# Strip matmuls of a decoder step that read and write their columns in backward order

## The reference

```python
h = rmsnorm(x, norm1_g)
z = h @ w_in                       # 2048 -> 18448 columns
u, cg, bg, q, k, v, o, gif, g_a, g_b = split(z)
a_out = bg * causal_dwconv(cg * u, state, w_shortconv)
hb = mlstm(q, k * DK ** -0.5, v, gates(gif), state)       # 8 heads
mix = sigmoid(g_a) * a_out + sigmoid(g_b) * sigmoid(o) * hb
x = x + mix @ w_out                # 2048 -> 2048
up = causal_dwconv(rmsnorm(x, norm2_g) @ w_up, state, w_ffconv)   # 2048 -> 11264
x = x + (silu(up[..., D_FF:]) * up[..., :D_FF]) @ w_down          # 5632 -> 2048
y = rmsnorm(x, norm_f_g)
```

## Time and profile before

| | before |
|---|---|
| runs | 1708.65 us median of 3 (1707.38 to 1709.73) |
| profiled execution, span | 1706.3 us |
| TensorE (PE) busy | 1695.1 us, 99% |
| VectorE (DVE) busy | 1200.1 us, 70% |
| ScalarE (ACT) busy | 766.5 us, 45% |
| GpSimd (POOL) busy | 479.6 us, 28% |
| read from and written to HBM | 305.09 MB and 12.78 MB |

### The profile page before, as it was taken

The page is one execution under the profiler, slowest core; times in us unless marked ns, Lnnn a source line. Parts: engine busy times, 40 slices in busy tenths (PEclk is TensorE's granted clock), DMA queues, the critical chain, the costliest instruction groups (busy, mean ns, idle before and its releaser), DMA issues.

```text
span 1706.3 us, 37177 instructions
## 1 busy us (share of the span) xinstructions
PE 1695.1 (99%) x13726; PEld 1688.7 (99%) x13726; DVE 1200.1 (70%) x1901; ACT 766.5 (45%) x916; POOL 479.6 (28%) x501
## 2 busy tenths in 40 slices
PE   9999999999999999999999999999999999999997
PEld 8999999999999999999999999999999999999997
DVE  5875957667595766759688877777555777777554
ACT  6545435354443535444444554544333334334443
POOL 4422414242141424215343222222000222222220
PEclk9999999999999999999999999999999999999999
DMA  8787786868778586877866666656666666666663
GB/s 204 183 230 197 201 212 155 225 162 231 188 198 212 156 226 163 230 189 199 196 178 182 185 175 175 180 173 173 183 181 181 181 178 179 176 180 177 183 176 119
DMA packets 591165, 318.80 MB, mean 187 GB/s; under 512 B 17684, under 2 KB 585988, under 8 KB 588988
## 3 DMA queue, kind: packets, MB, share of 16 engines
q1 hardware_dynamic: 578564, 292.99, 63.2%
q10 hardware_dynamic: 10448, 21.57, 4.7%
q0 software_dynamic: 2064, 2.92, 0.8%
HBM read 305.09 MB, written 12.78 MB: 186 GB/s over the span
## 4 chain that ended last, share of the span: by engine, by line
PE 99%; ACT 0%; POOL 0%; DVE 0%; issue 0%; ACTq 0%; POOLq 0%; DVEq 0%
PE strip L1528 32%; PE strip L1520 32%; PE strip L1524 32%; PE aux L1399 1%; PE aux L1407 1%; PE strip L1451 0%; PE aux L1581 0%; PE aux L1471 0%; PE strip L1464 0%; PE aux L1611 0%; PE aux L1610 0%; PE aux L1624 0%; PE strip L1399 0%; PE aux L1615 0%; PE aux L1608 0%; PE aux L1616 0%
## 5 line engine op out<-in xcount | busy, mean ns | idle before, releaser
L978 DVE TENSOR_TENSOR w_lo<-w_raw,w_hi 128x1024 fp32r<-128x1024 f32 x556 | 723.1, 1303 | 315.3 <-ACT w_hi L709 314.8
L709 ACT ACTIVATE w_hi<-w_raw 128x1024 fp32r<-128x1024 f32 x557 | 586.1, 1059 | 756.7 <-PE strip L1528 724.7
L1520 PE MATMUL strip<-xh,w_hi 128*128 128x268 f32 (+1 forms) x3424 | 493.1, 286 | 0.0
L1528 PE MATMUL strip<-xh,w_lo 128*128 128x268 f32 (+1 forms) x3424 | 492.4, 286 | 0.0
L1524 PE MATMUL strip<-xl,w_hi 128*128 128x268 f32 (+1 forms) x3424 | 492.0, 286 | 0.0
L1528 PEld LDWEIGHTS strip<-xh,w_lo 128*128 128x128 f32 x3424 | 449.4, 188 | 0.3
L1520 PEld LDWEIGHTS strip<-xh,w_hi 128*128 128x128 f32 x3424 | 449.4, 188 | 0.2
L1524 PEld LDWEIGHTS strip<-xl,w_hi 128*128 128x128 f32 x3424 | 449.4, 188 | 0.0
L680 POOL TENSOR_TENSOR gg<-sg,cz 128x264 f32<-128x264 f32 x44 | 57.1, 1297 | 415.8 <-ACT sg L923 415.8
L1520 PE MATMUL strip<-hh,w_hi 128*128 128x264 f32 x704 | 102.2, 286 | 0.0
L683 POOL TENSOR_TENSOR hid<-gg,cz 128x264 f32<-128x264 f32 x44 | 73.5, 1670 | 102.2 <-DVE cz L1327 102.2
(11 more groups left out here) (324 smaller groups left out, 1285.3 us busy)
## 6 DMA issues: line engine op xcount, KB each, us to landing
w_raw<-in_w_in SPq DMA_DIRECT2D x256, 512.0 KB, 4.4
w_raw<-in_w_up SPq DMA_DIRECT2D x176, 512.0 KB, 3.9
w_raw<-in_w_down SPq DMA_DIRECT2D x64, 512.0 KB, 3.9
w_raw<-in_w_out SPq DMA_DIRECT2D x32, 512.0 KB, 4.4
w_raw<-in_w_down SPq DMA_DIRECT2D x32, 384.0 KB, 3.3
out<-c_st ACTq DMA_DIRECT2D x8, 1024.0 KB, 7.2
c_st<-in_state_mlstm_C ACTq DMA_DIRECT2D x7, 1024.0 KB, 10.5
rb<-scratch_rows ACTq DMA_DIRECT2D x8, 270.0 KB, 5.0
```

Source lines behind the costliest of these rows:

```text
L709: act.activation(w_hi[:, slot, :], w_raw[:, slot, :], ACT.Copy).then_inc(hi_done, 1)
L978: v.tensor_tensor(w_lo[:, slot, :], w_raw[:, slot, :], w_hi[:, slot, :].bitcast(f32), ALU.subtract).then_inc(lo_done, 1)
L1520: pe.matmul(bank[b][:, 0:c1 - c0], w_hi[:, slot, w], rh[:, k0 + k, c0:c1], start=(first and k == 0), stop=False)
L1528: mm = pe.matmul(bank[b][:, 0:c1 - c0], w_lo[:, slot, w], rh[:, k0 + k, c0:c1], start=False, stop=(last and k == kk - 1))
```

## The change

In all matmuls of the strips, the moving operand and the output are given with a step of minus one: the instruction reads the last column of its moving rows first, and writes the last column of its output first. Each output column gets the same products as before. The stationary operand, the order of the instructions, waits and transfers are not changed, nor are the matmuls into auxiliary banks.

```diff
--- before.py
+++ after.py
@@ -1448,7 +1448,7 @@
                     pe.wait_ge(xl_done, k + 1)
                     w = slice(k % KU * P, (k % KU + 1) * P)
                     for t, xt in enumerate((xh, xl)):
-                        mm = pe.matmul(bank[s][:, 0:NT - c0], w_hi[:, 2 * s + k // KU, w], xt[:, k, c0:NT],
+                        mm = pe.matmul(bank[s][:, 0:NT - c0][:, ::-1], w_hi[:, 2 * s + k // KU, w], xt[:, k, c0:NT][:, ::-1],
                                        start=(k == 0 and t == 0), stop=False)
                 return mm
 
@@ -1461,8 +1461,8 @@
                     pe.wait_ge(lo_done, RING + 2 * (s + 1))
                 for k in range(lo, hi):
                     pe.wait_ge(xh_done, k + 1)
-                    mm = pe.matmul(bank[s][:, 0:NT - c0], w_lo[:, 2 * s + h, (k - h * KU) * P:(k - h * KU + 1) * P],
-                                   xh[:, k, c0:NT], start=False, stop=(last and k == KT - 1))
+                    mm = pe.matmul(bank[s][:, 0:NT - c0][:, ::-1], w_lo[:, 2 * s + h, (k - h * KU) * P:(k - h * KU + 1) * P],
+                                   xh[:, k, c0:NT][:, ::-1], start=False, stop=(last and k == KT - 1))
                 return mm
 
             def gates(lo, hi):
@@ -1517,15 +1517,15 @@
                         if at_k == k:
                             pe.wait_ge(sm, value)
                     w = slice(k * P, (k + 1) * P)
-                    pe.matmul(bank[b][:, 0:c1 - c0], w_hi[:, slot, w], rh[:, k0 + k, c0:c1],
+                    pe.matmul(bank[b][:, 0:c1 - c0][:, ::-1], w_hi[:, slot, w], rh[:, k0 + k, c0:c1][:, ::-1],
                               start=(first and k == 0), stop=False)
                 for k in range(kk):
                     w = slice(k * P, (k + 1) * P)
-                    pe.matmul(bank[b][:, 0:c1 - c0], w_hi[:, slot, w], rl[:, k0 + k, c0:c1], start=False, stop=False)
+                    pe.matmul(bank[b][:, 0:c1 - c0][:, ::-1], w_hi[:, slot, w], rl[:, k0 + k, c0:c1][:, ::-1], start=False, stop=False)
                 pe.wait_ge(lo_done, u + 1 + RING)
                 for k in range(kk):
                     w = slice(k * P, (k + 1) * P)
-                    mm = pe.matmul(bank[b][:, 0:c1 - c0], w_lo[:, slot, w], rh[:, k0 + k, c0:c1],
+                    mm = pe.matmul(bank[b][:, 0:c1 - c0][:, ::-1], w_lo[:, slot, w], rh[:, k0 + k, c0:c1][:, ::-1],
                                    start=False, stop=(last and k == kk - 1))
                 if frees:
                     mm.then_inc(unit_used, frees)
```

## The result

The changed kernel takes 1712.05 us, median of 14 runs (1711.08 to 1712.91); the kernel before took 1708.83 us beside it (14 runs, 1707.38 to 1710.89). The ratio is 1.0017, with a 95% interval of 1.001 to 1.0024: 3.2 us more. That is inside the 0.2% named as "no change", but close to its edge: the interval does not contain 1, and its upper end lies beyond the 0.2%.

The account below looks back on a forecast made before the run. The prediction took TensorE's pace from one strip matmul to the next as the bound; terms 0 + 0 + 0 left the span at 1706.3 us, so it forecast 1708.7 us for the runs, range 1,696 to 1,730 us.

Parts of the forecast that it names:

- no change: Whole kernel: time stays within 0.2%, 3.4 us, of the kernel before; chance 0.54.
- half rate: Rival, all strip matmuls: falling order handles one word at a time, in full 3,286 us; chance 0.20.
- upper bound of 119 ns a matmul: Strip matmuls: most a backward stream could add, falling to the rate of unrounded operands; 1,577 us over 13,248 matmuls.
- 8-byte rule: PSUM writes: lines hold 8 bytes and any access pattern that is not contiguous slows matmuls significantly.
- second reading: PSUM writes: every two consecutive elements should be contiguous; turned pairs stay in one line, so the sum would be 0.
- 0 + 0 + 0: Whole kernel: order between matmuls, edges and backward stream each cost 0, so the span stays at 1706.3 us.
- the turned stream itself: Strip matmuls' backward read and write: taken as 0, between a gain of at most 13 us and a 1,577 us cost.
- cover that I named: Strips of 264 to 268 columns: a cycle or two at a row's start may hide; at 280 it would show.
- small cost: Rival, 9,600 strip matmuls at 122 ns: each pays 2.1 ns, 20.2 us more, 1,729 us; chance 0.14.
- quick pace throughout: Rival: first up pass leaves 124 ns for 122, 5.2 us less, 1,703 us; with wide strips 1,696; chance 0.12.
- main step: Forecast of no change: strip starts 122 or 124 ns apart at 268 columns, 128.75 at 280, same 13,726 instructions.
- Edges: Strips' moving rows and banks: widths and starts are even, so backward reads cover the same word pairs; cost 0.

Follow-up runs that it names:

- output_only: Kernel before with only the strips' output columns written backwards, moving rows read forwards: 1708.71 us against 1708.68, ratio 1.0002 (0.9993 to 1.0011).

## Why the prediction was right, point by point

**The bound.** TensorE's row set the time before and after: it is busy for 99% of the span in both, and its list of waits is the same.

**No half rate.** The upper bound of 119 ns a matmul was not approached; the largest change of any stage is about 2 ns. The 8-byte rule that I weighed is thus settled for this case in the second reading: by the runs a backward write costs nothing, 1.0002 (0.9993 to 1.0011). The Trainium skill, page "Advanced Engine Details and Errata", section "PSUM Cachelines", asks that every two consecutive elements be contiguous, and the output_only trace agrees that a step of minus one meets that, with 121.7 ns in the output strips as before.

The 241 ns behind that upper bound was misread: it is the length of a piece of the chain divided by 12, and not a distance between starts. The twelve f32 matmuls and the first strip matmul behind them start here:

```profile
9.80 2.96 PE L1407 MATMUL aux<-acc,ones 128*128 128x266 f32 x12
...
12.40 0.48 PE L1451 MATMUL strip<-xh,w_hi 128*128 128x268 f32 x1
```

That is 2.60 / 12 = 217 ns, so the bound was about 95 ns a matmul, some 1,260 us in all. The rival stays as far off as it was.

**The sum 0 + 0 + 0.** It came out at 3.2 us, 0.24 ns a matmul, a hair under the 0.26 that I had set as its border. The term "the turned stream itself" was mis-sized as one number: it is +0.5 ns in the heads' strips behind the score matmuls, +0.35 in the wide strips, +2 in the output strips, -0.9 in the first up pass, +1.2 in the second, and +0.2 and 0 in the two passes of down strips. That the total is near zero is partly a cancelling of stages, and so far it was luck: without the 1.7 us that the first up pass gave back, the change would have cost 4.9 us, 0.29%. The cover that I named (cycles hidden at 264 to 268 columns) held only for 264, nearly. The row it was read from does not show a cover either: the transposes at 110 ns work on f32 operands, and if 266 such columns take 217 ns, 128 come to 104 ns (an estimate), so their columns may explain most of it. And the column per cycle was read from the slower of the two paces at 268 columns; from 122.1 ns the step to 280 columns is 0.55 ns a column.

**The two small rivals.** I gave them as cases that exclude each other, a small cost (0.14) and the quick pace throughout (0.12). Each happened in part, in different stages: the second up pass and the output strips became slower; the first up pass became quicker, though at 123.3 ns and not at 122. So did the strips ahead of the score matmuls, 0.99 us for 8 before; in the changed kernel's chain they read:

```profile
152.82 0.98 PE strip L1528 x8
```

Nor did the sign come that I had named for the main step, starts of 268 columns 122 or 124 ns apart: the turned strips have paces of their own, 122.5 and 123.3. The sentence on which the second rival was turned down, that the pace changes where the instruction mix changes and the turn leaves that alone, failed: the same mix leads turned strips into other paces, and in the second head before the pace changes where the mix does not.

**Edges.** "Reading the same pairs of words" was not enough for a forward read: two words' shift alone moved it by 0.8 ns. But it is not what the backward read pays for: turned, the same shift left 124.0 ns.

**What is shown and what is open.** Shown: the read alone makes the difference; each shape and direction has a few paces (268 columns: 122.0 and 124.2 forward, 122.5 and 123.3 turned); a stage keeps its pace for hundreds of matmuls; one wide f32r matmul can change it, and so can a stop of about 0.1 us, behind which two executions of one program differ. Not shown: what in TensorE or its reads makes the paces, and what decides at a stage's entry. Neither the f32 matmul alone, nor the place of the first word alone, nor the type of the last auxiliary matmul alone does.

## What to carry to other kernels

In this kernel (f32r operands, 264 to 280 columns) reading and writing backwards loses no rate: the write cost nothing that could be measured, and the read moves the pace by -0.9 to +2 ns of 122. Where TensorE is the bound and its row is dense, compare the distance between starts stage by stage for the same shape before looking for anything bigger: two stages of one shape at two paces differed by 4.8 us here (262.51 and 257.73), and one extra matmul of 0.12 us won back 4.2 of them. How far such a gain holds elsewhere is not shown: two words' shift of an operand or a stop of 0.1 us moved paces too. A mean over the kernel hides such paces, and a change that "does nothing" should be read by stage, since it may be gains and losses that cancel.

## What was not expected of the hardware

A dense row of the same instruction, with the same addresses and clock, has discrete paces that last: 124.2 against 122.1 ns for 268 columns in two passes of identical work, repeated in a second profile to the tenth. And one transpose can end the quick one: before, in the first head, 8 strip matmuls take 0.98 us ahead of it and 0.99 to 1.00 behind it, for the next 30 us.

```profile
59.32 1.14 PE L1524 MATMUL strip<-xl,w_hi 128*128 128x268 f32 x8
60.30 1.14 PE L1528 MATMUL strip<-xh,w_lo 128*128 128x268 f32 x8
61.27 0.27 PE L1399 MATMUL aux<-ident,tails 128*24 128x128 f32 x1
...
62.36 1.15 PE L1524 MATMUL strip<-xl,w_hi 128*128 128x268 f32 x8
63.36 1.16 PE L1528 MATMUL strip<-xh,w_lo 128*128 128x268 f32 x8
```
